# One core of Trainium2: the first output tile placed between the gates' first pair and the pooled products, with weight highs, head seam and pool groups in another order

## Chip, cores and metric

One core of one Trainium2 chip. The metric is the device time in microseconds (us) of one execution. A profiled execution gives the rows; the other times are of runs without a profile.

## What is computed

One step of a streaming encoder layer, in fp32, on 1024 prompt tokens and 32 sample tokens. Cut to what matters:

```
x += 0.5 * post(SwiGLU_1(pre(x)))            # FFN 1, d_ff 2816
h = pre(x); z = h @ W_in                     # q|f|i|og|u|gA|gB, d_model 1024
yA = up_A(gnorm(HGRN2(q, f, i)) * silu(og))  # 8 heads of 128, chunks of 64
yB = up_B(scale * groupwise_linear(trailing_mean_w(u) - u)), w in (2, 4, 8, 16)
x += post(W_out(sigmoid(gA) * yA + sigmoid(gB) * yB))
x += 0.5 * post(SwiGLU_2(pre(x)))            # FFN 2
x += post(sigmoid(pre(x) @ W_pg) * (p @ W_pp))
```

Outputs are the new x and the new recurrent and pooling states, for prompt and sample.

## The kernel before

**Tiles.** Activations lie feature-major, 8 tiles of 128 features, 1056 tokens in four groups `g` of N = 264. An fp32 product is made of f16 halves: each operand is split in a high and a low, and three matmuls of 128x128 by 264 columns (high-high, high-low, low-high; lines 818 to 820 and 849 to 852) stand for one. TensorE issues 20814 matmuls in all.

**Weights** come in units of four 128x128 tiles into a ring of slots. SyncE loads them in the order of use (`load`, `load_pair` at L650), once the slot is free. ScalarE scales a unit by 32 and makes its high half; GpSimd makes its low half. For plain tiles these are `prep` (L1096: scale L1107, high L1109) and GpSimd's `split` (low L719). For pairs they are `scale` (L1144, four raw units), `to_high` (L1154, L1162) and GpSimd's `pair` (L721), which also adds and subtracts raw units (sums L736, lows L732). `first_highs` (L1171) is `to_high` for the first pair of a stage, whose slots were last used by the stage before.

**Plain tiles and pairs.** `turn` (L798) makes plain output tiles, a job per token group. `pair` (L832) makes two columns of output tiles at once by a scheme of seven products in place of eight: each product `k` in two token halves `e` of 12 matmuls, 168 matmuls per pair. Its right-hand operands are sums of activation blocks, `t`, which VectorE adds (`t_block`, L1909), ScalarE rounds to a high half (`t_high`, L1185, L1191) and VectorE subtracts to a low (`t_lows`, L1919). Its results are put together from the seven products in PSUM banks: ScalarE copies some banks (`chain_copies`, L1371), VectorE adds the rest (L1936 in the FFNs, L2027 in the mixer). Each read releases its bank (`bank_read`), and a matmul group waits for the bank that it will fill.

**Stages, in the order of TensorE.** FFN up: 16 plain tiles (first tiles), then 20 pairs; FFN down. Mixer: first head's value, output gate, q and f tiles (head0), 16 pairs for the rest and for the pooling input u, in which the head before is worked on: transposes of values and keys (L931), scores, updates, outputs (L986) stand between products (`head_hooks`, L999). Then pair 0 of the gates, 16 pool tiles of one product each (4 banks), the first outputs (tile 0: 8 blocks by 4 groups, 96 matmuls, from the heads; tile 1: 4 blocks by 4 groups, from the pools), then seven turns of pair and outputs. Then W_out, FFN 2, and the last gate (ple).

**What sets the order.** Each engine has its own program, written out by hand; they meet in semaphores with counted values. The class `Plan` works out banks, uses and slots for each job (`job`, L261), and so what each wait counts to. An engine takes its instructions in order, so an instruction whose input is late holds back all behind it.

**What the change touches.**
- ScalarE: the start (L1673 to L1699: `squares`, `prep`, `norm`, `h_high`, `silus` with its table load at L1141), `up(f)` (L1193), the seam from head0 to the pairs (L1712 to L1726), `head_turn` (L1462), `gates` (L1579) with `pooled_high` (L1564, copy at L1569) and the pooled products' high copies (L1627). `ln_exp_tables` loads the tables for ln and exp.
- VectorE: the start (`h_split` L1778, `square_sum` L1771, `first_squares`, `products`), the seam (L2403 to L2414; `head0_silus` at L2016, `decay_keys` at L2107, `head_turn` L2142 with the scan at L2150 and the key operand at L2125), `gates` (L2322) with `pooling` (L2254, a group of one window; its adds are L2275 for windows 4 and up and L2265 for window 2), `pooled_low` (L2286), the last head's norm (L2112) and low (L2120), `mixed` (L2292, low halves of the pooled products, L2297), `gated` and `joins` (L2303, L2348).
- TensorE: the norms' places in `up(0)` (L1019), `keys_and_values` (L992), and the order of gates, pools and outs (L1042 to L1044).

The order of the pool groups is `POOL_ORDER` (3, 2, 1, 0) for windows 16, 8, 4, 2.

## Time and profile before

| | |
|---|---|
| runs | 2442.74, 2446.56, 2446.6 us; median 2446.56 |
| profiled execution | 2445.24 us |
| its span on the core | 2443.4 us, 54106 instructions |
| mean granted clock of TensorE | 0.983 of full speed |
| busy share | TensorE 96%, weight loads 82%, VectorE 54%, ScalarE 47%, GpSimd 45% |
| the chain that ended last | TensorE 74%, VectorE 9%, issue 8%, GpSimd 5%, ScalarE 3% |
| DMA | 147.26 MB, mean 60 GB/s |

The span is from the first to the last recorded instruction. The granted clock 1.00 is 2.4 GHz, 0.50 is 1.2 GHz. PE is TensorE, DVE VectorE, ACT ScalarE, POOL GpSimd. "L849 <- DVE work L1936" means that the instruction of line 849 waited for a VectorE instruction of line 1936 on the buffer `work`.

### The profile page before, as it was taken

Reading aid. Unit: us, or ns where it says so; the run is one execution under the profiler, and the core shown is the slowest. Engines: PE = TensorE matmul, PEld = TensorE weight load, DVE = VectorE, ACT = ScalarE, POOL = GpSimd, SP = SyncE. Lnnn points to the kernel's source line nnn. Section 1 sums busy time; section 2 is a strip of 40 time slices with the busy share of each in tenths; the row PEclk is TensorE's granted clock in tenths of the full one; section 3 lists DMA queues with packets and bytes.
Section 4 is the critical chain, followed back from the end, with each engine's and each line's share of the span. In section 5 each row is a group of like instructions: output and inputs, shape, how many; then the busy total and the mean of one; then the engine's idle time right before and its main releaser. Section 6 shows DMA issues by size and latency. Waiting matters only on the chain.

```text
span 2443.4 us, 54106 instructions
## 1 busy us (share of the span) xinstructions
PE 2339.7 (96%) x20814; PEld 2004.0 (82%) x20814; DVE 1317.9 (54%) x2273; ACT 1155.7 (47%) x2087; POOL 1111.7 (45%) x881
## 2 busy tenths in 40 slices
PE   7899999999997999999979999988999999999988
PEld 5688888888886888888758888877888888888876
DVE  7655555400189777778952332387666666000755
ACT  6343344333465666666444443653333333334575
POOL 2676777422214555554635443314677776223110
PEclk9999999999998999999989999999999999999999
DMA  3122112322220111111101122321111122321202
GB/s 128 41 59 56 52 56 60 121 53 74 59 85 19 47 46 39 39 51 38 55 23 44 60 60 81 117 80 31 56 52 52 53 58 73 119 70 49 66 18 72
DMA packets 98519, 147.26 MB, mean 60 GB/s; under 512 B 10480, under 2 KB 43504, under 8 KB 98416
## 3 DMA queue, kind: packets, MB, share of 16 engines
q1 hardware_dynamic: 70352, 121.14, 17.1%
q10 hardware_dynamic: 28064, 24.69, 3.1%
q8 instruction: 72, 1.18, 0.2%
q14 instruction: 31, 0.25, 0.0%
HBM read 131.70 MB, written 14.09 MB: 60 GB/s over the span
## 4 chain that ended last, share of the span: by engine, by line
PE 74%; DVE 9%; issue 8%; POOL 5%; ACT 3%; DMA 1%; DVEq 0%; POOLq 0%; ACTq 0%; SPq 0%
PE bank L818 12%; PE bank L849 12%; PE bank L819 12%; PE bank L820 12%; PE bank L852 12%; PE bank L851 12%; POOL ring L732 3%; DVE hid L1974 2%; DVE work L1972 1%; POOL ring L736 1%; DMA ring<-weights 1%; PE bank L975 1%; DVE hid L1785 1%; ACT ring L1148 1%; PE bank L986 1%
## 5 line engine op out<-in xcount | busy, mean ns | idle before, releaser
L849 PE MATMUL bank<-ops,ring 128*128 128x264 f16 x3584 | 994.8, 278 | 34.2 <-DVE work L1936 14.7
L851 PE MATMUL bank<-ops,ring 128*128 128x264 f16 x3584 | 994.0, 277 | 0.0
L852 PE MATMUL bank<-ops,ring 128*128 128x264 f16 x3584 | 994.0, 277 | 0.0
L732 POOL TENSOR_TENSOR ring<-ring 128x512 f16<-128x512 f32 x384 | 484.1, 1279 | 280.7 <-ACT ring L1162 280.7
L818 PE MATMUL bank<-hid,ring 128*128 128x264 f16 x2124 | 587.3, 277 | 0.0
L819 PE MATMUL bank<-hid,ring 128*128 128x264 f16 x2124 | 587.1, 276 | 0.0
L820 PE MATMUL bank<-hid,ring 128*128 128x264 f16 x2124 | 587.0, 276 | 0.0
L719 POOL TENSOR_TENSOR ring<-wtmp,ring 128x512 f16<-128x512 f32 x173 | 203.9, 1181 | 667.4 <-ACT ring L1109 666.3
L849 PEld LDWEIGHTS bank<-ops,ring 128*128 128x128 f16 x3584 | 353.2, 99 | 100.9 <-issue 25.6
L1162 ACT ACTIVATE ring<-ring 128x512 f16<-128x512 f32 x384 | 226.6, 622 | 405.5 <-POOL ring L736 404.0
L852 PEld LDWEIGHTS bank<-ops,ring 128*128 128x128 f16 x3584 | 352.3, 98 | 54.4
L851 PEld LDWEIGHTS bank<-ops,ring 128*128 128x128 f16 x3584 | 352.5, 98 | 52.9
L1811 DVE TENSOR_TENSOR u<-u,work 128x264 f32<-128x264 f32 x112 | 58.3, 521 | 403.7 <-ACT work L1228 402.6
L819 PEld LDWEIGHTS bank<-hid,ring 128*128 128x128 f16 x2124 | 208.2, 98 | 32.8
L818 PEld LDWEIGHTS bank<-hid,ring 128*128 128x128 f16 x2124 | 208.2, 98 | 32.2 <-DVE hid L2297 0.5
L820 PEld LDWEIGHTS bank<-hid,ring 128*128 128x128 f16 x2124 | 208.2, 98 | 31.5
L736 POOL TENSOR_TENSOR wtmp<-ring 128x512 f32<-128x512 f32 x64 | 84.1, 1313 | 306.0 <-ACT ring L1148 306.0
L1148 ACT ACTIVATE ring<-ring 128x512 f32<-128x512 f32 x256 | 148.9, 621 | 152.9 <-DMA ring<-weights 152.6
L818 PE MATMUL bank<-ops,ring 128*128 128x264 f16 x640 | 182.7, 285 | 21.7 <-DVE hid L2016 5.6
L819 PE MATMUL bank<-ops,ring 128*128 128x264 f16 x640 | 182.6, 285 | 0.0
L820 PE MATMUL bank<-ops,ring 128*128 128x264 f16 x640 | 182.4, 285 | 0.0
L736 POOL TENSOR_TENSOR ring<-ring 128x512 f32<-128x512 f32 x128 | 173.3, 1354 | 0.0
(179 smaller groups left out, 2855.7 us busy)
## 6 DMA issues: line engine op xcount, KB each, us to landing
ring<-weights SPq DMA_DIRECT2D x429, 256.0 KB, 2.7
hid<-xT SPq DMA_DIRECT2D x8, 528.0 KB, 8.3
hid<-out_x ACTq DMA_DIRECT2D x8, 528.0 KB, 7.6
out_x<-hid ACTq DMA_DIRECT2D x8, 528.0 KB, 4.2
ops<-xT ACTq DMA_DIRECT2D x6, 528.0 KB, 7.1
out_x<-ops ACTq DMA_DIRECT2D x6, 528.0 KB, 4.2
ops<-out_x ACTq DMA_DIRECT2D x6, 528.0 KB, 6.5
out_x<-ops SPq DMA_DIRECT2D x12, 264.0 KB, 2.2
```

The source lines that it names most:

```text
L719: nc.gpsimd.tensor_tensor(low(slot), wtmp[:, u % 2, :], high(slot), ALU.subtract).then_inc(unit_ready, 1)
L732: nc.gpsimd.tensor_tensor(low(slot), weight_source(name, k), high(slot), ALU.subtract)\
L736: nc.gpsimd.tensor_tensor(out, in0, in1, op).then_inc(wsum_ready, 1)
L818: nc.tensor.matmul(out, whi, rhs(t, k, g, 0), start=(k == 0), stop=False)
L819: nc.tensor.matmul(out, whi, rhs(t, k, g, 1), start=False, stop=False)
L820: mm = nc.tensor.matmul(out, wlo, rhs(t, k, g, 0), start=False, stop=end)
L849: nc.tensor.matmul(out, whi, xhi, start=(kk == 0 and fresh(name, k)), stop=False, skip_group_check=True)
L851: nc.tensor.matmul(out, whi, xlo, start=False, stop=False, skip_group_check=True)
L852: mm = nc.tensor.matmul(out, wlo, xhi, start=False, stop=end, skip_group_check=True)
L1148: nc.scalar.activation(raw(slot), raw(slot), ACT.Copy, scale=WS).then_inc(scaled, 1)
L1162: nc.scalar.activation(high(slot), weight_source(name, k), ACT.Copy).then_inc(whi_ready, 1)
L1811: V_.tensor_tensor(ssq(g), ssq(g), pair_buf[:, n % 2, :], ALU.add).then_inc(ysq_added, 1)
```

## The change

It reorders; no matmul, product or transfer is added or removed, but table loads are (at the start `ln_exp_tables` is also called between silu 0 and silu 1). By part:

- **Gates, TensorE:** pair 0, output tile 0, pools, output tile 1, where it was pair 0, pools, both output tiles. The pools keep their four banks; `Plan.job` counts the uses anew.
- **Gates, ScalarE:** the second and third chain copies stand ahead of most weight preparations; the pooled products' copies stand ahead of the weight highs 3 to 6.
- **Gates, VectorE:** window 2 before window 4; the last head's norm and low ahead of the window-4 group; tile 0's gated product ahead of the pooled lows.
- **FFN up, ScalarE:** weight highs 2 to 6 ahead of late t highs, in both FFNs.
- **Heads' seam:** VectorE's t blocks are cut in two by `head0_silus`; decay keys ahead of the last t lows; weight highs 5 and 6 moved into `head_turn(1)`; value transposes wait for the values alone; the last head unit's order.
- **Start:** preparations and the splits of the first token groups in another order; the second t block's squares of group 2 on VectorE instead of ScalarE; the norms' places.

The diff, cut:

```diff
 HG_FIRST = {k: HG_PIECES.index(k) for k in dict.fromkeys(HG_PIECES)}
-POOL_ORDER = (3, 2, 1, 0)
-HEAD_UNITS = ((4, 5, 2, 3), (2, 3, -4, -3), (6, 7, 4, 5), (-2, -1, -4, -3))
+POOL_ORDER = (3, 2, 0, 1)
+HEAD_UNITS = ((4, 5, 2, 3), (2, 3, -4, -3), (6, 7, 4, 5), (-4, -3, -2, -1))
...
 b = self.banks(name)[pos % STAGES[name]["banks"]]
+if name == "pools":
+    return b, self.base[name][b] + pos // STAGES[name]["banks"] + 1
+if name == "outs" and isinstance(i, int) and i == 0 and pos < G:
+    return b, self.base["pools"][b]
...
             pe.wait_ge(bank_read[b], uses)
-    def turn(name, i, kind, rhs, ready=None, hooks=None, order=None):
+    def turn(name, i, kind, rhs, ready=None, hooks=None, order=None, ts=None):
...
         for pos, (t, g) in enumerate(jobs_of(name, kind)):
+            if ts and t not in ts:
+                continue
...
         pe.wait_ge(operand_ready, head * 8 + n)
-    def keys_and_values(h):
-        pe.wait_ge(k_ready, h)
-        for e in range(2):
-            b, uses = plan.product("heads", h * 2 - 3, 6, e)
+    def values(h):
+        pe.wait_ge(pads_set, 1)
+        for g in range(G):
+            b, uses = plan.head0_job(0, g)
             pe.wait_ge(bank_read[b], uses + 1)
+        for k in (3, 6):
+            for e in range(2):
+                b, uses = plan.product("heads", h * 2 - 3, k, e)
+                pe.wait_ge(bank_read[b], uses + 1)
...
         return [{
-            (0, 1): [lambda: keys_and_values(h), lambda: head_transposes(hh, "vT", V)],
+            (0, 1): [lambda: values(h), lambda: head_transposes(hh, "vT", V)],
...
     norm(0)
-    up(0, {(1, 4): calls(1), (2, 4): calls(2), (5, 0): calls(3)})
+    up(0, {(2, 2): calls(1), (3, 4): calls(2), (7, 0): calls(3)})
...
     pair("gates", 0)
+    turn("outs", 0, "M", out_rhs, first_out_ready, ts=(0,))
     turn("pools", 0, "M", pool_rhs, pool_ready, order=POOL_ORDER)
-    turn("outs", 0, "M", out_rhs, first_out_ready)
+    turn("outs", 0, "M", out_rhs, first_out_ready, ts=(1,))
...
         return freed
-    def t_high(p, n, at):
+    def t_high(p, n, at, es=range(2)):
...
             act.wait_ge(x_saved[g], saves(1, g))
-        for e in range(2):
+        for e in es:
...
         t_high(2 * f, 2, (2, 4))
-        high0(2)
-        silus(f, (6, 7))
-        t_high(2 * f, 3, (5, 6))
-        high0(3)
+        silus(f, (6,))
+        high0(3, 4)
+        silus(f, (7,))
+        t_high(2 * f, 3, (5, 6), (0,))
+        high0(5, 6)
+        t_high(2 * f, 3, (5, 6), (1,))
         t_high(2 * f, 1, (1, 3))
-        high0(4)
         t_high(2 * f, 4, (7, 8))
-        high0(5, 6)
...
             silus(1, (2, 3))
-            first_highs(UPS[1][1])(0, 1)
+            first_highs(UPS[1][1])(0, 1, 2)
...
         exps_32(hh)
-        if not (isinstance(h, int) and h == 1):
+        if isinstance(h, int) and h == 1:
+            first_highs("heads")(5, 6)
+        else:
...
             .then_inc(pool_stored[j], 16)
+    def mixed_high(t):
+        for g in range(G):
+            b, uses = plan.job("pools", 0, t * G + g)
+            act.wait_ge(bank_full[b], uses + 1)
+            nc.scalar.activation(hid[:, MIX0 + POOL_ORDER[t], g, 0:N], bank[b][:, 0:N], ACT.Copy,
+                                 scale=pscale(POOL_ORDER[t])).then_inc(mixed_hi_ready, 1)
...
                     to_high("gates", m + 1, ks, freed)
+            first = isinstance(m, int) and m == 0
             chain_copies("gates", m, 0)
-            if isinstance(m, int) and m == 0:
+            if first:
                 first_highs("gates")(5, 6)
-            prep("outs", m, 0, 1, 2)
-            if not last:
+                chain_copies("gates", m, 2)
+                prep("outs", m, 0)
+                pooled_high(1)
+                prep("outs", m, 1, 2)
+                chain_copies("gates", m, 4)
+                pooled_high(2)
+                onorm_high(HEADS - 1, W[3])
                 scale("gates", m + 1)
-            if isinstance(m, int) and m == 0:
-                pooled_high(1)
-            chain_copies("gates", m, 2)
-            ahead(0, 1)
-            chain_copies("gates", m, 4)
-            if isinstance(m, int) and m == 0:
-                pooled_high(2)
-                pooled_high(3)
-                onorm_high(HEADS - 1, W[3])
+                ahead(0, 1)
             else:
+                prep("outs", m, 0, 1, 2)
+                if not last:
+                    scale("gates", m + 1)
+                chain_copies("gates", m, 2)
+                ahead(0, 1)
+                chain_copies("gates", m, 4)
...
             ahead(2)
+            if first:
+                pooled_high(3)
...
             nc.scalar.activation(dst_b, gb_all, ACT.Sigmoid).then_inc(gate_ready, 1)
+            if first:
+                for t in range(4):
+                    mixed_high(t)
...
         gate_turn(0, TMP_FIRST[0][:, 0:T], TMP_FIRST[1][:, 0:T])
-        for n, (t, g) in enumerate((t, g) for t in range(4) for g in range(G)):
-            b, uses = plan.job("pools", 0, n)
-            act.wait_ge(bank_full[b], uses + 1)
-            nc.scalar.activation(hid[:, MIX0 + POOL_ORDER[t], g, 0:N], bank[b][:, 0:N], ACT.Copy,
-                                 scale=pscale(POOL_ORDER[t])).then_inc(mixed_hi_ready, 1)
...
     norm(0)
-    prep("ffn1_up0", 0, 2, 3)
+    prep("ffn1_up0", 0, 2)
     h_high(0, 0)
+    prep("ffn1_up0", 0, 3, 4)
     squares(0, 1)
-    prep("ffn1_up0", 0, 4)
-    squares(0, 2)
+    prep("ffn1_up0", 0, 5, 6, 7)
     norm(1)
-    prep("ffn1_up0", 0, 5)
     h_high(0, 1)
-    prep("ffn1_up0", 0, 6)
+    silus(0, (0,))
     squares(0, 3)
-    prep("ffn1_up0", 0, 7)
+    ln_exp_tables()
     norm(2)
-    silus(0, (0,))
...
     silus(0, (2, 3))
-    first_highs(UPS[0][1])(0, 1)
+    first_highs(UPS[0][1])(0, 1, 2)
...
     head0_evac(3)
+    t_high(1, 4, (7, 8))
+    high0(4)
     ln_exp_tables()
-    high0(4)
-    t_high(1, 4, (7, 8))
-    high0(5, 6)
...
         sq = hq(p, g)
-        dve.wait_ge(squares_ready, SQUARE_PARTS * (G * p + g + 1))
+        if p or g != 2:
+            dve.wait_ge(squares_ready, SQUARE_PARTS * (G * p + g + (0 if p or g > 2 else 1)))
...
                 .then_inc(h_ready, 1)
-        ahead = 2 if c == 0 else PARTS
+        ahead = min(c + 1, 2) if p == 0 else PARTS
...
                          pooled[j][:, :, 0:N], ALU.subtract).then_inc(pooled_ready, 1)
-    def mixed():
-        for n, (t, g) in enumerate((t, g) for t in range(4) for g in range(G)):
-            b, _ = plan.job("pools", 0, n)
+    def mixed_low(t):
+        for g in range(G):
+            n = t * G + g
+            b, uses = plan.job("pools", 0, n)
...
                                     in1=dst[:, 0:N], op0=ALU.mult, op1=ALU.subtract).then_inc(bank_read[b], 1)
-        dve.wait_ge(bank_read[b], plan.job("pools", 0, n)[1] + 1)
+        return b, uses
+    def mixed(t):
+        b, uses = mixed_low(t)
+        dve.wait_ge(bank_read[b], uses + 1)
...
         pooling(2, 2 * HEADS - 1, 1, 5)
+        onorm(HEADS - 1, W[3], LAST_RMS)
         sums_b_odd("gates", 0, lambda g: gcols(gb_all, g))
+        pooled_low(2)
+        onorm_low(HEADS - 1, W[3])
         pooling(3, 2 * HEADS - 1, 3, 6)
-        onorm(HEADS - 1, W[3], LAST_RMS)
-        pooled_low(2)
...
         pooled_low(3)
-        onorm_low(HEADS - 1, W[3])
-        mixed()
+        first_gated(0, lambda g: gcols(TMP_FIRST[0], g))
+        for t in range(3):
+            mixed_low(t)
+        mixed(3)
...
             gate_sums(m)
+            first_gated(m, lambda g: hidv[:, TMP0, g, :])
...
         sums_b_even("gates", m, lambda g: gcols(gb_all, g))
-    def joins(m, a, s, dst):
+    def first_gated(m, a):
...
             gated(m, 0, g, a(g))
+    def joins(m, a, s, dst):
...
     h_split(0, 0)
+    for n, ks in enumerate(parts_of(SQUARE_PARTS)):
+        x = xk(0, 2, ks.start, ks.stop)
+        dve.wait_ge(x_loaded[2][n], 16)
+        step(V_.tensor_tensor(hq(0, 2)[:, ks, :], x, x, ALU.mult))
     first_squares(1)
-    first_squares(2)
+    square_sum(0, 2)
     h_split(0, 1)
+    products(0, (0,))
     first_squares(3)
-    products(0, (0,))
...
     step(V_.memset(smask.rearrange("p (c t) -> p c t", t=C)[:, :, 0], 0.0))
-    t_block(1, (1, 2))
+    t_block(1, (1, 2), (0,))
     head0_silus(1)
+    t_block(1, (1, 2), (1,))
     t_lows(1, 2)
-    t_block(1, (3,))
+    t_block(1, (3,), (0,))
     head0_silus(2)
+    t_block(1, (3,), (1,))
...
     head0_silus(3)
-    t_lows(1, 4)
...
     decay_keys(0)
+    t_lows(1, 4)
```

## Rows read from the trace of the kernel before

**Rows 1.** The page, part 1: busy time, share of the span, instructions

```profile
PE 2339.7 (96%) x20814; PEld 2004.0 (82%) x20814; DVE 1317.9 (54%) x2273; ACT 1155.7 (47%) x2087; POOL 1111.7 (45%) x881
```

**Rows 2.** Waits of TensorE, whole span: us in total, times, longest us

```profile
PE bank L849 <- DVE work L1936: 14.7, 21, 4.6
PE bank L818 <- DVE hid L2297: 12.1, 1, 12.1
PE bank L849 <- POOL ring L732: 11.9, 4, 3.9
...
PE bank L931 <- DVE hid L2107: 5.8, 1, 5.8
PE bank L818 <- DVE hid L2016: 5.6, 1, 5.6
...
PE bank L849 <- ACT work L1371: 5.2, 8, 2.5
...
PE bank L849 <- DVE work L2027: 2.3, 2, 1.7
```

**Rows 3.** Windows, mid-FFN 1 and 2: us, PE, PEld, DVE, ACT, POOL, clock, DMA, GB/s

```profile
130.00:450.00 320.00, 320.00 (x2847) 278.33 (x2845) 178.37 (x337) 128.23 (x221) 225.24 (x188) 1.00 0.21 60
1731.00:2051.00 320.00, 315.54 (x2783) 270.75 (x2781) 201.38 (x331) 120.92 (x215) 232.37 (x183) 1.00 0.20 56
```

**Rows 4.** Windows: the start, after FFN 1's seam, gates, pools, FFN 2's seam

```profile
0.00:70.30 70.30, 55.11 (x409) 44.38 (x410) 52.02 (x91) 44.99 (x70) 18.77 (x18) 0.93 0.34 115
108.90:114.80 5.90, 5.90 (x28) 4.04 (x29) 2.33 (x7) 2.28 (x4) 3.18 (x3) 0.50 0.14 44
1216.60:1280.00 63.40, 46.53 (x368) 37.42 (x366) 36.83 (x63) 28.11 (x52) 22.23 (x16) 0.87 0.10 30
1256.00:1261.70 5.70, 5.64 (x26) 3.91 (x27) 4.45 (x11) 4.11 (x10) 0.93 (x1) 0.50 0.01 3
1710.80:1714.00 3.20, 3.14 (x28) 2.75 (x29) 2.21 (x7) 1.30 (x3) 0.43 (x1) 1.00 0.31 87
```

**Rows 5.** Timeline of ACT, gates: start, us, line, op, [idle before <- releaser]

```profile
1227.33 2.17 ACT L1148 ACTIVATE ring<-ring 128x512 f32<-128x512 f32 x4
...
1255.01 1.58 ACT L1627 ACTIVATE hid<-bank,col 128x264 f16<-128x264 f32 x4
```

**Rows 6.** Timeline of DVE, gates

```profile
1232.19 4.37 DVE L2275 TENSOR_TENSOR hid<-hid 128x1085 f32<-128x1085 f32 x2
...
1240.10 1.23 DVE L2265 TENSOR_TENSOR hid<-hid 128x1023 f32<-128x1023 f32 x1
...
1255.51 1.69 DVE L2297 SCALAR_TENSOR_TENSOR hid<-bank,col,hid 128x264 f16<-128x264 f32 x4 [8.35 <-ACT hid L1627]
```

**Rows 7.** Timeline of ACT, seams from first tiles to pairs in both FFNs

```profile
82.20 2.25 ACT L1191 ACTIVATE ops<-hid 128x1056 f16<-128x1056 f32 x2 [5.45 <-DVE hid L1909]
...
91.27 0.63 ACT L1148 ACTIVATE ring<-ring 128x512 f32<-128x512 f32 x1 [4.22 <-DMA ring<-weights]
...
99.98 0.63 ACT L1169 ACTIVATE work<-work 128x528 f32<-128x528 f32 x1
...
1693.31 0.63 ACT L1148 ACTIVATE ring<-ring 128x512 f32<-128x512 f32 x1 [5.92 <-DMA ring<-weights]
```

**Rows 8.** Timeline of DVE, FFN 1, first pair

```profile
108.30 0.76 DVE L1936 COPY work<-bank 128x264 f32<-128x264 f32 x2
```

**Rows 9.** Timeline of DVE, heads' seam

```profile
734.57 7.03 DVE L1909 TENSOR_TENSOR hid<-hid 128x1056 f32<-128x1056 f32 x4
...
761.13 3.58 DVE L1919 TENSOR_TENSOR ops<-hid,ops 128x1056 f16<-128x1056 f32 x2 [1.56 <-ACT ops L1191]
...
767.55 2.42 DVE L2150 TENSOR_TENSOR_SCAN hid<-u,hid 128x1088 f32<-128x1088 bf16 x1 [1.27 <-ACT hid L1408]
...
774.57 1.27 DVE L2125 TENSOR_TENSOR hid<-hid 128x1088 f32<-128x1088 f32 x1
```

**Rows 10.** Timeline of ACT, start

```profile
48.65 1.28 ACT L1141 ACT_TABLE_LOAD   x1
```

## The prediction made before the change was run

> **What bounds the kernel now.** I read the page first: TensorE is busy for 2339.7 us, 96% of the span [rows 1], so only what keeps it waiting or slow can be won; no matmul is added or removed. The list of its waits comes next [rows 2]. The largest single one, 12.1 us, is for the VectorE line L2297 (low halves of the mixed pool products). Two more kinds lie in the same stage: 2.5 us at most for a ScalarE chain copy (L1371), and 2.3 us in two waits for L2027. The waits of 11.9 us for GpSimd's L732 and of 14.7 us for VectorE's L1936 lie where the FFNs go from their first tiles to their pairs; 5.8 us (L2107) and 5.6 us (L2016) lie where the heads begin. Third, the windows at mid-FFN [rows 3]: in 320 us the first FFN issues 2847 matmuls without a pause and the second only 2783. A matmul is 320/2847 = 0.1124 us; a pair of 168 takes 18.9 us in FFN 1 and 18.9 x 2847/2783 = 19.3 us in FFN 2. Fourth, the granted clock [rows 4]: after the long waits TensorE works at 0.50 (1.2 GHz), where each busy us costs 0.5 us. So a stall has two prices.
>
> **Gates (products of pair 0, pools, first outs).** Before, this takes 1216.6 to 1280.0, 63.4 us [rows 4]. Its 360 matmuls (14x12 + 16x3 + 4x24 + 4x12) need 40.5 us, so 22.9 us are lost: 16.9 in waits (12.1 + 2.5 + 2.3) and 6.0 in slow clock.
> - ScalarE before: three weight preparations, four scalings (2.17 us, row 1227.33 [rows 5]) and a pooled copy stand ahead of the copies of product 2, so product 4 starts 2.5 us late. The change puts these copies first; one preparation of 1.3 us and a pooled copy of 1.1 follow, then two more preparations. They end near 1230, just before product 4's first half does. The 2.5 and its slow clock go.
> - VectorE before: the window-4 pool group (its adds alone 4.37 us, row 1232.19 [rows 6]) stands ahead of the late sums of product 3's bank. Now the window-2 group, with one difference of 1.23 us (row 1240.10 [rows 6]), comes first: 1.7 us go, I keep 0.3. The 0.54 us wait behind the window-8 group stays.
> - The 12.1 us: the pool products start at once but only four banks exist, and the copies that free them come on ScalarE after seven weight highs, at 1255.01 [rows 5]. After the change TensorE does the first output tile first, 96 matmuls, 10.8 us, from 1236.4 to 1247.2. It needs the last head's split: the norm and its low half move ahead of the window-4 group and end near 1236.1, product index 7 wants it at 1237. The third pooled copy and the window-4 group (5 to 7 us of VectorE) lie under the 10.8 us.
> - Then the pools. Each tile needs a 0.49 us ScalarE copy and a VectorE op of the same size, at a pitch of 0.4 (row 1255.51 [rows 6]), against 0.34 us on TensorE. From the first tile's end 1.1 us pass to the first bank, 16 x 0.4 to the last: the second output tile starts near 1254.8, not 1252.6. Price 2.3 us.
> Sum: 22.9 - 0.5 - 0.3 - 2.3 = 19.8; I take **19.5**, bounds 15 (head split late, or slow clock in the pools) and 21. Queues: SyncE gets the pool unit and the outs units in the same order; the pool weight slots are loaded long before.
>
> **FFN seams.** Before, the chain in FFN 1 is: the second-block copies (L1191) end at 84.45; two highs follow, whose lows free the last raw slot; its load lands and is scaled at 91.27 [rows 7]; GpSimd's sums take 7.5 us; the silu is at 99.98 [rows 7]; VectorE then makes the hidden tile and copies the next product at 108.30 [rows 8]. TensorE waits 3.9, 1.2 and 4.6 us. With highs 3 to 6 moved ahead, slots are free and loaded before 84; the four scalings (2.1 us) run at once, with less GpSimd contention in the t blocks about 1 us earlier: scaled by 85.3, not 91.9. The whole chain moves 6.7 us. TensorE is then early: it stalls at most 1 us for the first weights of pair 1, and 4.7 us for L1936. So the last wait stays, and with it its slow clock (6 us at 0.50 before [rows 4], 3 us lost); I take it alike. Whether the start is worth more is below; with its slow clock I take **5.8** for start and seam of FFN 1, bounds 2 and 8.
> In FFN 2 the order is the same, but its load landed later (scaled from 1693.31 [rows 7]), so the chain moves 8.3 us. Its last wait was only 3.0 us and the clock stayed full (1710.8 to 1714.0 at 1.00 [rows 4]). I see in this why its pairs take 19.3 us: VectorE's hidden tile then falls on GpSimd's lows at once, L1936 is late in each pair (8 us over the FFN). FFN 1, put back 3 us by its slow clock, runs clear of it. With a wait of 4.7 us FFN 2 should get the slow clock (-3 us) and afterwards FFN 1's pace (+8.1 = 18 x 0.45). Sum 8.3 - 3.0 + 8.1 = **13.4**, bounds 6 and 16.
>
> **Heads' seam.** VectorE does four t sums, 7.03 us, before the silus that free TensorE's bank [rows 9]. Two stay ahead, 3.5 us go. The rest of the t chain hangs on GpSimd's sums and comes only some 1 us earlier. The first head's value transposes no longer wait for L2107: 5.8 us go at that place. But the key transposes wait for the operand at 774.57, which comes from decay keys, log, scan (767.55 [rows 9]). The decay keys now precede the last two lows (3.58 us [rows 9]), and two highs leave ScalarE's way: the scan starts at 762 to 763, the operand is done near 771.3 instead of 775.9. TensorE is there at 766.3: a wait of 5 us takes the place of the other two, and slow clock after it, 2.8 us. 4.6 - 2.8 = **1.8**, bounds 0 and 6. In the seven looped turns the added waits are for reads long done; TensorE shows no wait there but the chain copies of 0.2 to 0.5 us: nothing. A cover gone would cost up to 1 us a turn.
>
> **Start.** Earlier lows start TensorE 1.3 us sooner, and preparations put first remove its waits for the weights; it would reach the second group 5 us earlier. But ScalarE now has two more table loads (1.28 us each, row 48.65 [rows 10]) and all of h's copies later, so silu 2 ends near 53.7, not 50.3. Tile 10 wants its bank at 70.3 - 6 x 2.7 = 54.1 before [rows 4], at 50.6 now: it waits 3 us. Gain 0.4, perhaps minus 1.7 of slow clock. The Trainium skill, "ScalarE: Activation LUTs", What happens when an exp ACTIVATE runs, gives a table load about 2.7 us; at that the start alone would lose 2.5 us more, while the row says 1.28.
>
> **Sum.** 19.5 + 5.8 + 13.4 + 1.8 = 40.5 us. The profiled execution took 2445.2 (span 2443.4), 1.3 below the median of 2446.56; differences carry over: 2446.6 - 40.5 = **2406**.
>
> **Rivals.**
> - *FFN 2 keeps its slow pace* (the stall is short or the clock stays full): 8.3 - 1.2 = 7 instead of 13.4, or FFN 1 falls into it as well; 2413. For it: this is what FFN 2 does now. Against: every wait of 3.9 us or more here was followed by slow clock. Chance 0.20.
> - *Seams give nothing*, each wait moved to the next link with its clock; only gates: 2425. For: three of my seam sums already end in such a wait. 0.09.
> - *The first output tile waits for the last head or bank*, so nothing is filled: 2446 within 0.2%. Against: its operands are ready before in my walk. 0.03.
> - *Slower: GpSimd and VectorE collide in every FFN pair.* Place: GpSimd's five lows and sum against VectorE's hidden tile. Ops of 1.25 us take up to 2.2 when they meet (7.03 for four [rows 9]). Had all five met, the weight loop would be 18.4 + 5 = 23 us against 18.9; it decides once the loop exceeds the present pace by 1.1 us a pair (38 pairs eat 40 us), fully met about 2560. Against: rows 3 show 19.3 at worst. 0.04. The Trainium skill, "SBUF — State Buffer", SBUF: two separate sides, says that VectorE ops with two SBUF inputs and GpSimd's lock a shared port pair for a whole instruction; by that alone each of the five could wait a full op.
> - *The table load at the page's price*: 2409; 0.02. The remaining 0.02 is a gain above 50.
>
> **Numbers.** Forecast 0.60. Likeliest 2406, own range 2398 to 2411. The range takes in the slow-pace case and most of the third: 2396 to 2423. Over 0.2% (5 us, about what a measurement tells) faster: 0.60 + 0.20 + 0.09 + 0.02 + 0.02 = 0.93; same 0.03; slower 0.04.
>
> **What would show it.** Gates: no wait for L2297 over 1 us; pair 0 to pair 1 about 44 us. FFN seams: no wait for L732 over 1 us, one wait of 4 to 5 us for L1936 in each, both followed by 0.50; then 2847 matmuls in 320 us in both. Heads: value transposes without a wait, key transposes late by about 5. Start: tile 10 waits some 3 us. Wrong it would be if GpSimd's lows in the pairs lengthen, if head 7's split is what TensorE waits for at the first output tile, or if clock below 1 shows where no wait stands.

## The result and the profile after

The changed kernel takes 2424.64 us (median of 4 runs, 2423.38 to 2426.86) against 2446.58 (2442.74 to 2448.64): a ratio of 0.9915, 95% interval 0.9899 to 0.9930. That is 21.9 us faster where 40.5 were forecast, and 1.6 us above the upper end of the range. The profiled execution took 2425.5 us, its span is 2423.6.

The page of the changed kernel, part 1, answers to [rows 1]:

```profile
PE 2336.5 (96%) x20814; PEld 1998.0 (82%) x20814; DVE 1361.7 (56%) x2275; ACT 1151.5 (48%) x2087; POOL 1131.4 (47%) x881
```

VectorE has two instructions more and is busy 43.8 us longer; GpSimd has none more and is busy 19.7 us longer. The same work takes longer; why is the subject of the section on the two rhythms. TensorE's waits of the changed kernel (us in total, times, longest) answer to [rows 2]:

```profile
PE bank L856 <- DVE work L1962: 14.1, 37, 2.4
PE bank L856 <- DVE work L1982: 8.1, 2, 4.3
...
PE bank L825 <- ACT work L1154: 5.2, 2, 2.9
...
PE bank L938 <- DVE hid L2151: 4.0, 1, 4.0
...
PE bank L825 <- DVE hid L2342: 1.0, 1, 1.0
```

L1962 is L1936 of before (VectorE's copy of product 0 of the next pair), L1982 VectorE's sum of product 4, L1154 the silus of the first tiles, L2342 the new line of tile 0's gated product. The 12.1 us for the pooled lows, the 2.5 for L1371 and the 11.9 for GpSimd's lows are gone. But the copy of product 0 is now waited for 37 times, not 21. The windows answer to [rows 3] (both FFNs, shifted as the FFNs are) and to the gates' window of [rows 4]; columns as there:

```profile
130.00:450.00 320.00, 314.84 (x2777) 270.06 (x2776) 201.91 (x330) 120.00 (x213) 231.66 (x182) 1.00 0.20 56
1711.00:2031.00 320.00, 316.09 (x2788) 271.15 (x2786) 201.09 (x330) 121.90 (x216) 233.61 (x184) 1.00 0.19 57
```

```profile
1223.10:1267.40 44.30, 41.04 (x353) 32.76 (x352) 38.70 (x60) 26.63 (x50) 22.55 (x16) 1.00 0.13 41
```

FFN 1 had 2847 matmuls in 320 us; it now has 2777, as few as FFN 2. The gates' stretch takes 44.3 us in place of 63.4, at full clock.

TensorE has 20814 matmuls in both kernels, and outside the gates in the same order. So the n-th can be set against the n-th, and the difference of their starts says where time went:

```
part (numbers of TensorE's matmuls)        forecast   traces (changed minus before)
start (0 to 504)                            -0.4        +5.3
FFN 1's seam (504 to 672)                   -5.4        -6.9
FFN 1's pairs (672 to 3864)                  0         +10.1
heads' seam (6048 to 7392)                  -1.8        -2.1
gates, pools, outs (10584 to 11256)        -19.5       -19.1
FFN 2's seam (14448 to 14616)               -5.3        -6.5
FFN 2's pairs (14616 to 17640)              -8.1        -0.6
rest                                         0          +0.1
sum                                        -40.5       -19.8
```

Four of seven terms are right within 1.5 us. What fails is the pairs of both FFNs (17.6 us in all) and the start (5.7 us). The rest is a sum of two parts that no term had: 1.7 us less between the gates and FFN 2 (matmuls 11256 to 14448) and 1.6 us more behind FFN 2's pairs; in both a stretch at 0.50 is there in one of the two executions and missing or shorter in the other.

Each row comes from one execution of each kernel. Where the other kernels below hold the same code, their executions tell how far such a number moves. The start of matmul 504 lies between 85.5 and 87.2 us in the six with the changed start, and between 81.0 and 81.6 in the five with the start as before. The heads' seam wins 1.0 to 4.0 us. The gates' part wins 19.1 us where the clock stays at 1.00 behind a wait of 3.0 us at the heads' end (the changed kernel, e5, e6, e9, e11, e13 to e15), 17.4 where it falls to 0.50 for 3.4 us there (e1, e3, e10, e12), and 16.1 to 16.2 where it falls for 6.8 us (e2, e7, e8).

### The profile page after: what moved, and what is told of

Its sections match the earlier page's. It is cut to its first block, busy times and chain, and to the rows that moved or that the text cites. A ratio compares the mean times of both kernels' runs of the same rounds, so it can differ in the third digit from the quotient of the medians.

```text
span 2423.6 us, 54141 instructions
## 1 busy us (share of the span) xinstructions
PE 2336.5 (96%) x20814; PEld 1998.0 (82%) x20814; DVE 1361.7 (56%) x2275; ACT 1151.5 (48%) x2087; POOL 1131.4 (47%) x881
## 4 chain that ended last, share of the span: by engine, by line
PE 69%; DVE 13%; issue 9%; POOL 4%; ACT 3%; DMA 1%; DVEq 1%; POOLq 0%; ACTq 0%; SPq 0%
PE bank L825 11%; PE bank L826 11%; PE bank L827 11%; PE bank L856 11%; PE bank L859 10%; PE bank L858 10%; DVE hid L2000 4%; DVE work L1998 3%; POOL ring L737 2%; DVE hid L1811 1%; POOL ring L741 1%; PE bank L982 1%; DMA ring<-weights 1%; ACT ring L1161 1%; PE bank L938 1%
## 5 line engine op out<-in xcount | busy, mean ns | idle before, releaser
L737 POOL TENSOR_TENSOR ring<-ring 128x512 f16<-128x512 f32 x384 | 490.8, 1297 | 261.5 <-ACT ring L1175 261.5
```

What stands on the lines that cost most here:

```text
L737: nc.gpsimd.tensor_tensor(low(slot), weight_source(name, k), high(slot), ALU.subtract)\
```

## Two rhythms of the FFN pairs

One pair in the fast rhythm, kernel before, FFN 1: timelines of VectorE and of GpSimd (start, us, line and operation).

```profile
274.32 0.70 DVE L1972 SCALAR_TENSOR_TENSOR work<-work 128x528 f32<-128x528 f32 x1
275.18 1.15 DVE L1974 TENSOR_SCALAR hid<-work 128x528 f32 x1 [0.16 <-DVE work L1972]
276.47 1.44 DVE L1975 TENSOR_TENSOR hid<-work,hid 128x528 f32 x1
277.83 0.69 DVE L1972 SCALAR_TENSOR_TENSOR work<-work 128x528 f32<-128x528 f32 x1
278.68 0.44 DVE L1974 TENSOR_SCALAR hid<-work 128x528 f32 x1
279.25 0.71 DVE L1975 TENSOR_TENSOR hid<-work,hid 128x528 f32 x1
```

```profile
274.82 2.53 POOL L732 TENSOR_TENSOR ring<-ring 128x512 f16<-128x512 f32 x2 [0.74 <-ACT ring L1162]
281.12 1.27 POOL L736 TENSOR_TENSOR wtmp<-ring 128x512 f32<-128x512 f32 x1 [3.78 <-ACT ring L1148]
```

These six VectorE operations make the hidden tile, in two halves; GpSimd's are the lows and sums of the next pair's weights. The hidden tile takes 5.64 us, its second half falls into GpSimd's pause, and the next sum of raw weights starts 6.8 us after the tile's start (281.12 - 274.32). This span is called the distance from here on. The loop that makes the weights of the next pair (load, ScalarE's scaling and highs, GpSimd's sums and lows) is called the weights' loop. The same pair in the changed kernel:

```profile
276.61 1.02 DVE L1998 SCALAR_TENSOR_TENSOR work<-work 128x528 f32<-128x528 f32 x1
277.79 1.14 DVE L2000 TENSOR_SCALAR hid<-work 128x528 f32 x1 [0.16 <-DVE work L1998]
279.08 1.55 DVE L2001 TENSOR_TENSOR hid<-work,hid 128x528 f32 x1
...
282.70 1.44 DVE L2001 TENSOR_TENSOR hid<-work,hid 128x528 f32 x1
284.06 0.76 DVE L1962 COPY work<-bank 128x264 f32<-128x264 f32 x2
```

```profile
277.02 1.62 POOL L737 TENSOR_TENSOR ring<-wtmp,ring 128x512 f16<-128x512 f32 x1
278.60 1.45 POOL L741 TENSOR_TENSOR ring<-ring 128x512 f32<-128x512 f32 x1
280.80 2.77 POOL L737 TENSOR_TENSOR ring<-ring 128x512 f16<-128x512 f32 x2 [0.74 <-ACT ring L1175]
287.34 1.26 POOL L741 TENSOR_TENSOR wtmp<-ring 128x512 f32<-128x512 f32 x1 [3.77 <-ACT ring L1161]
```

```profile
284.61 0.28 PE L856 MATMUL bank<-ops,ring 128*128 128x264 f16 x1 [0.28 <-DVE work L1962]
```

Both halves now meet GpSimd. The tile takes 7.53 us, the copy behind it comes late, and TensorE waits for it. The distance is 10.7 us. An operation of 0.44 us takes 1.14 and one of 0.71 takes 1.55 when they meet; GpSimd's low takes 1.62, not 1.16. The operations at 277.79 and 279.08 end 0.3 and 0.6 us after the GpSimd operation beside each has ended (278.64, 280.05). This is so in every pair looked at: in the changed kernel from 130 to 440 us all 32 operations of L2000 end 0.29 us after the GpSimd operation under which they began, and all 32 of L2001 end 0.56 to 0.57 us after it. Each is its undisturbed time (0.44 and 0.71 us) less about 0.15 us. The Trainium skill, "SBUF — State Buffer", SBUF: two separate sides, calls the shared port pair an exclusive lock, held for a whole instruction; these ends agree with it.

The numbers of the distance and the tile in all four FFN runs:

```
                    distance   hidden tile   pair
before, FFN 1       6.7-6.9     5.64         18.90 (from pair 2)
before, FFN 2       10.5-10.9   7.4-7.8      19.2-19.6
changed, FFN 1      10.5-10.9   7.4-7.7      19.2-19.5
changed, FFN 2      10.5-10.9   7.4-7.7      19.2-19.6
```

What sets the distance? In the kernel before, FFN 1 starts at 10.9 too; 22.48 us pass to its second hidden tile, which stands at 6.8. In between lie the wait of 4.63 us for the copy (104.23) and 6.8 us at 0.50 (from 108.01), both behind the start of the first hidden tile (100.64). The reading is that they held TensorE and VectorE back, and not the weights, which had been started. In the changed kernel the long wait is for product 4 (4.34 us at 88.90, clock 0.50 from 92.31), ahead of the first silu. The silus and the weights' highs share ScalarE's queue, so both loops would shift together.

By the matmuls' numbers the wait stands where one stood before. At matmul 526 TensorE waited 3.89 us for GpSimd's lows; now it waits 4.34 us there for VectorE. The waits of 1.22 us at matmul 574 and 4.63 us at 646 are gone (0.17 us are left at 646). In FFN 2, matmul 14478 waited 3.89 us for the lows and now waits 3.72 us for VectorE; 2.87 us at 14526 are gone, and 2.95 us at 14598 became 1.74. VectorE came late because its own queue was full: from 60 us to 93.5 us no gap in it is over 0.04 us, and the fourth t block (L1935) and its lows (L1945) stand ahead of the sum:

```profile
87.41 2.41 DVE L1935 TENSOR_TENSOR hid<-hid 128x1056 f32<-128x1056 f32 x2
89.74 0.76 DVE L1977 TENSOR_TENSOR work<-bank,work 128x264 f32<-128x264 f32 x2
90.42 2.41 DVE L1945 TENSOR_TENSOR ops<-hid,ops 128x1056 f16<-128x1056 f32 x2
92.76 0.76 DVE L1982 TENSOR_TENSOR work<-bank,work 128x264 f32<-128x264 f32 x2
```

The theory: a delay of TensorE behind pair 0's silus decides the rhythm. The rival: the order of the weight highs does.

## Experiments on the pairs

Each ratio is to the kernel before, measured beside the run. The changed kernel has 0.9915 [0.9899, 0.9930]; of the experiments only e5 and e8 have an interval that lies wholly below this one. The total time of the others that are built on the changed kernel does not tell them from it, and the argument rests on their traces; e4 is built on the kernel before and compared with that.

**e3: a delay added.** 32 matmuls, written over by the next one; nothing else changes.

```diff
-                pair(rest, 0, t_wait(p))
+                pair(rest, 0, t_wait(p), pad={(6, 0): 32})
...
+                        for _ in range((pad or {}).get((k, e), 0)):
+                            nc.tensor.matmul(out, ring[:, slot, 0:P], ops[:, e, k, 0, 0:N], start=True, stop=False,
```

> The changed kernel with 32 more matmuls (3.6 us) ahead of product 6 of pair 0, in both FFNs, written over by the next one: a single delay of TensorE and of VectorE's hidden tile against the weights' loop. Theory of two rhythms: the distance from the hidden tile to GpSimd's next sum falls from 10.7 to 7.1 us or less and stays there, the pairs go at 18.9 us and not 19.4, and the time falls by 2 x (0.5 x 19 - 3.6), about 11 us, to 2413. Rival (the pace comes from the order of the weight highs or from the slots): the pairs stay at 19.4 us and the time rises by up to 7.2 us, to 2431.8.

2416.75 us (2413.64 to 2426.20), ratio 0.9892 [0.9862, 0.9923]; windows of e3:

```profile
130.00:450.00 320.00, 320.00 (x2847) 278.33 (x2845) 188.73 (x339) 123.07 (x218) 231.36 (x187) 1.00 0.20 59
1711.00:2031.00 320.00, 320.00 (x2847) 278.33 (x2845) 189.27 (x340) 127.33 (x225) 231.80 (x188) 1.00 0.21 61
```

The median is 7.9 us under the changed kernel's; one of the four runs (2426.20) lies among the changed kernel's, and the intervals overlap. The trace is plain: with 64 matmuls more both FFNs go without a pause, at 18.90 us per pair. The order of the weight highs is the changed kernel's, so the rival falls. The distance starts at 7.6 us, where 7.1 or less was expected, and creeps to 8.5 by FFN 1's pair 17; the tile grows with it from 5.7 to 6.9 us. So this distance does not hold by itself. The runs spread over 12.6 us.

**e4: the same delay in the kernel before, FFN 2 alone.**

> The kernel before with the same 32 matmuls in pair 0 of FFN 2 alone. Theory of two rhythms: FFN 2 goes at 18.9 us per pair as FFN 1 does; -8.1 + 3.6, about 4.5 us less: 2442. Rival: FFN 2 stays at 19.35 us per pair and the time rises to 2450.

2444.8 us (10 runs, 2439.76 to 2448.29), ratio 0.9992 [0.9981, 1.0004]: no difference that counts. In the profiled execution (2441.73 us) the delay works: the distance is 7.8 and grows to 9.9 at pair 15, the pairs take 18.90 up to there and 19.3 behind it. Between the same matmuls FFN 2's seam takes 1.7 us more and its pairs 5.9 less, 4.2 in all. The median of the ten runs does not show this. That the fast rhythm was lost earlier in others would explain it, but they have no trace.

**e11: the seams' order undone** (weight highs 3 to 6 in both FFNs as before, rest as changed).

> The changed kernel with the order of weight highs at both FFNs' seams as before. Theory: the seams cost 6.9 and 6.5 us again, but the wait of 4.6 us for the copy of pair 1 and the slow clock behind it come back behind the first hidden tile, delay TensorE against the weights' loop, and both FFNs go at 18.9 us per pair: 10 and 8 us less. Net 4 to 5 us less than the changed kernel, about 2420. Rival (the rhythm does not hang on where the seam's wait falls): both stay at 19.4 us and the time rises to 2438.

2422.97 us, ratio 0.9915 [0.9898, 0.9932]: the ratio of the changed kernel itself. The medians differ by 1.7 us, where 4 to 5 were expected and the runs spread over 4.8. Its waits:

```profile
PE bank L856 <- DVE work L1961: 11.7, 3, 4.6
PE bank L856 <- POOL ring L737: 7.8, 2, 3.9
```

Both waits of 4.6 us are back behind the first hidden tile, and both FFNs go at 18.90: FFN 1 at distance 7.8, lost in the last three pairs; FFN 2 from 7.8 down to 6.7, where it holds. From nearly one distance it may go either way. (The same holds in e1 below: its FFN 1, with the code of the kernel before, stands at 7.95 in its second pair and not at 6.8, and loses the fast rhythm after pair 15.)

What holds 6.7 is a wait of ScalarE. In the kernel before, FFN 1, the first silu of each pair waits 0.2 to 0.4 us for TensorE's product (through VectorE's L1959):

```profile
270.45 0.64 ACT L1169 ACTIVATE work<-work 128x528 f32<-128x528 f32 x1 [0.32 <-DVE work L1959]
```

e11's FFN 2 shows the same once it stands at 6.7. At distances from 7.6 to 8.5 (e3 in both FFNs, e11's FFN 1) and at 10.7 (the slow rhythm in both kernels) the silus of these pairs wait for nothing, so the weights' loop is free to drift there.

By the matmuls' numbers the seam gives back 6.6 us and FFN 1's pairs win 8.0. So the seams' part of the change, which won 13.4 us at its place, is worth about nothing as a whole.

**e1: the gates' part alone,** on the kernel before.

> The kernel before with the gates' part alone (order of TensorE, ScalarE and VectorE there, pool groups, last head unit). If the gates' gain is its own, TensorE's time is alike up to the gates and 19 to 19.6 us less behind them: about 2427.5 us. Rival: the gates' gain hangs on where the heads end, and the last head's order costs in the heads what it gives here; then under 15 us.

2421.53 us, ratio 0.9902 [0.9874, 0.9930]: one part of the change does as much as all of it. At the gates it wins 17.4 us, less than the 19.1 in the whole; the 1.7 between them is a stretch of 3.4 us at 0.50 at the heads' end (from 1213.13), which comes in this execution and not in the other, behind the same wait of 3.0 us. The 6 us under the expected 2427.5 come from FFN 2, whose code is that of the kernel before: at matmul 14598 it waited 4.62 us for the copy, not 2.95, the clock was at 0.50 for 6.8 us, and its pairs went at 18.90, 7.6 us less.

**e6: VectorE's copies of the next pair between the halves of the hidden tile.**

> The changed kernel with VectorE's copies of the next pair's product 0 between the two halves of the hidden tile, in both FFNs, the weights' loop as it was. TensorE then no longer waits for those copies. If the copy behind the hidden tile is the whole bound, all pairs go at 18.9 us: about 2406. If the weights' loop is a bound of its own at 19.4 us, the distance from hidden tile to sum grows by 0.45 us per pair from 10.7, and after some ten pairs TensorE waits for GpSimd's lows in each pair instead: about 2415. Rival (neither counts): 2424.6.

2426.18 us, ratio 0.9920 [0.9897, 0.9943]. In the looped pairs no copy is waited for any more, but L2002 (product 4) is:

```profile
PE bank L856 <- DVE work L2002: 14.8, 29, 4.3
```

The distance stays at 10.6 to 10.9, it does not grow, and the pairs take 19.3: the tile now starts when the silu ends (276.61), and the silu stands in ScalarE's queue behind weight high 3, which waited 4.0 us for GpSimd's sum (to 275.35). So the weights' loop looks like a bound of its own, which reaches TensorE by the silu and VectorE, not by the lows as I had expected. e5 puts this to the test.

**e5: a shorter weights' loop.**

```diff
-                    scale(name, i + 1)
-                    to_high(name, i + 1, range(4), product_before(name, i))
+                    scale(name, i + 1, (0, 2, 1))
+                    to_high(name, i + 1, (0, 1), product_before(name, i))
+                    scale(name, i + 1, (3,))
+                    to_high(name, i + 1, (2, 3), product_before(name, i))
...
+                if early:
+                    lo(0)
+                    lo(1)
                 pool.wait_ge(scaled, p * RAWS + (sums + 4))
```

> The changed kernel with a shorter weights' loop in the FFN pairs: ScalarE makes highs 0 and 1 before it scales the last raw unit, and GpSimd their lows before its two sums, so 2.3 us of GpSimd's work lie under the 3.7 us in which it waits for the last load. No delay is added. If the slow rhythm lives on a weights' loop that takes 19.4 us by itself, the loop now takes about 17.1, runs up against the silus, and all pairs go at 18.9 us with a hidden tile of 5.6 to 6.5 us: 19 x 0.5 in each FFN, about 2406 us. Rival: VectorE's hidden tile is slowed wherever the loop stands and TensorE still waits 0.45 us for the copy in each pair: 2424.6.

2414.5 us, ratio 0.9875 [0.9852, 0.9898]. ScalarE and GpSimd in e5:

```profile
270.15 0.64 ACT L1187 ACTIVATE work<-work 128x528 f32<-128x528 f32 x1 [1.20 <-DVE work L1992]
```

```profile
277.77 1.48 POOL L737 TENSOR_TENSOR ring<-ring 128x512 f16<-128x512 f32 x1 [0.72 <-ACT ring L1180]
279.86 1.55 POOL L737 TENSOR_TENSOR ring<-ring 128x512 f16<-128x512 f32 x1 [0.61 <-ACT ring L1180]
281.38 1.26 POOL L741 TENSOR_TENSOR wtmp<-ring 128x512 f32<-128x512 f32 x1
```

The silu now waits 1.2 us for TensorE's product (through L1992) in each pair, so the loop has slack and cannot drift, as at 6.7 above but with more room: from pair 3 on the distance is 7.34 to 7.36, the tile 6.37, the pair 18.90, in both FFNs. Lows 0 and 1 lie ahead of the sum. It wins 10.1 us on the changed kernel and not 18.6: the first two pairs still go at 19.4 to 19.6, the wait for the copy at pair 1 is 2.3 us, and by the matmuls' numbers the pairs of FFN 1 and FFN 2 give 8.0 and 7.0 us, less 0.6 at each seam.

**e8: e5 with the start as before.**

> The shorter weights' loop together with the start as before. If both gains are their own, 4.4 us (the start) and 2 x 9.5 us (the rhythm) go from 2424.6: about 2401, below both kernels. Rival: one eats the other (the first pair's wait grows by what the start gives), 2406.

2408.14 us (2406.40 to 2409.11), ratio 0.9845 [0.9822, 0.9868]: 16.5 us less than the changed kernel, the best of all, though 7 us short of the expected 2401, as e5 was. The two gains do not eat each other (10.1 and 3.9 alone, 16.5 together).

## Experiments on the start and the heads

**e2: the start as before.**

> The changed kernel with the start as before (ScalarE's and VectorE's start and the places of the norms undone). Theory A: the start's 5.3 us are a loss of their own; TensorE ends its first tiles 5 us earlier and the time falls to about 2419.5. Rival B: the first pair hangs on VectorE's t chain anyway; then the wait at FFN 1's first pair (4.3 us now) grows by most of 5 us and the time stays within 1.5 us of 2424.6.

2420.7 us, ratio 0.9894 [0.9871, 0.9917]: 3.9 us less. TensorE reaches matmul 504 4.8 us earlier, and the wait at the first pair does not grow (3.2 us, not 4.3): the loss is its own.

What in it costs? ScalarE in the changed kernel at the silus:

```profile
46.46 0.64 ACT L1141 ACTIVATE ops<-hid 128x528 f16<-128x528 f32 x1 [1.16 <-DVE hid L1811]
47.12 1.28 ACT L1154 ACT_TABLE_LOAD   x1
...
54.95 0.64 ACT L1141 ACTIVATE ops<-hid 128x528 f16<-128x528 f32 x1 [0.77 <-DVE hid L1811]
55.62 1.28 ACT L1154 ACT_TABLE_LOAD   x1
56.91 0.67 ACT L1154 ACTIVATE work<-bank 128x264 f32<-128x264 f32 x2
```

Silus 2 and 3 stood at 49.94 before, behind the load of [rows 10]; now at 56.91. Six kernels take the start apart (all else as changed; the numbers are TensorE's start of matmul 504 in us, 86.26 in the changed kernel, 80.99 in the one before; by the spread given above, differences under some 1.5 us say nothing):

**e7: silu 0 and its tables back.**

> The changed kernel with silu 0 behind the third norm again and without the added table call; the rest of the start stays as changed. If the start's 5.3 us come from the two added table loads (1.28 us each) and what they push back, TensorE's waits for the silus (2.3 and 2.9 us) fall to one of under 2 us and 4 to 5 us come back at the end of the first tiles: 2420. If they come from the late copies of h, less than 2 us come back: 2423 or more. The pairs stay at 19.4 us in both.

87.7, and 2426.95 us (0.9926 [0.9903, 0.9948]). The loads alone are not it.

**e9: group 1's norm early,** though group 2's squares and sum still stand ahead of group 1's split on VectorE, so the copies of h came only 0.6 us earlier (31.54).

> The changed kernel with token group 1's norm early again: its squares ahead of preparations 3 and 4, its sum on VectorE ahead of group 2's squares, the norms' places on TensorE as before; silus, tables and group 2's squares on VectorE stay as changed. If the start's loss comes from the copies of h, which run 5.5 us late from group 1 on (32.14 against 26.61), 4 us or more come back before the first pair and the time falls to 2420 or less. If it comes from the silus' places and their tables, the copies come early but TensorE waits for a silu as before: 2424.

87.7, and 2427.0 us (0.9930 [0.9914, 0.9947]); the edit missed its aim, TensorE waited 5.2 us for GpSimd's lows.

**e12: group 1 wholly first.**

> The changed kernel with token group 1 wholly ahead of group 2 at the start: on VectorE its sum and its split stand ahead of group 2's squares and sum (5.9 us in the last try, where they stood between the two), on ScalarE its squares and norm ahead of the preparations. If those 5.9 us are what makes the copies of h late, group 1's copies start at 27 to 28 us and not at 32.1, and TensorE ends its first tiles 3 to 5 us earlier: 2420 to 2421. Rival: the preparations, now behind, hold the first tile's later units, TensorE waits for GpSimd's lows (L724) instead, as it did for 5.2 us in the last try, and under 1 us comes back.

87.7, and 2425.44 us (0.9918 [0.9902, 0.9935]): its rival holds. The copies start as wanted, but GpSimd's two lows take 4.23 us beside VectorE's splits and squares, and TensorE waits 6.6 us for them:

```profile
27.82 0.64 ACT L1141 ACTIVATE ops<-hid 128x528 f16<-128x528 f32 x1 [0.95 <-DVE hid L1811]
```

```profile
32.74 4.23 POOL L724 TENSOR_TENSOR ring<-wtmp,ring 128x512 f16<-128x512 f32 x2 [7.83 <-ACT ring L1122]
```

**e13: group 2's squares back on ScalarE. e14: silu 0 and tables too. e15: the norms' places too.**

> The changed kernel with group 2's squares on ScalarE again (right behind group 1's) and VectorE's start as before. If VectorE's added squares hold the start back, TensorE reaches the middle of pair 0 (its 504th matmul, 86.3 us) 3 us earlier or more; if the loss hangs on silu 0 and the tables together with them, only the next kernel shows it, and here it is under 1.5 us.

> As the last one, and silu 0 behind the third norm again without the added table call. If both edits together hold the loss (each alone is hidden by the other), 4 us or more of the 5.3 come back at the same matmul; if it is the preparations or the norms' places, no more than in the last one.

> As the last one, and the norms at their old places on TensorE; only the order of ScalarE's weight preparations is still the changed one. If the late norms hold the copies of h back, the rest of the 5.3 us comes back here; if the preparations ahead of norm 1 do it, TensorE still comes 2 us late or more and only the whole undo (81.0 to 81.5 us at the same matmul) has it.

85.8, 83.7 and 84.0, and 2425.99, 2422.25 and 2423.86 us (3, 3 and 3 runs; 0.9913 [0.9891, 0.9936], 0.9896 [0.9873, 0.9918], 0.9899 [0.9876, 0.9921]). So about half of the loss sits in the squares and the silu's tables together, each of which alone gives nothing that can be told from the spread; the norms' places give nothing; the other half (83.7 to 84.0 against 81.5 in e2) is in what is left, the preparations put ahead of group 1's norm and VectorE's order of full tiles and lows (the line `ahead = min(c + 1, 2)`, which the expectations of e13 and e15 overlook). Which of the two it is stays open.

**e10: the heads' seam as before.**

> The changed kernel with the heads' seam as before. TensorE's time from the start of the first head tiles to the second head grows by 2 us (what the two traces show between the same matmuls), nothing else moves: 2426.6. Rival: the seam's waits are filled by what is late anyway, no difference over 0.5 us.

2426.99 us (0.9934 [0.9918, 0.9951]). By the matmuls' numbers 1.9 us come back from 6048 to 6384, as expected; the 2.3 of the medians is of the size of the runs' spread. But against the executions of e2, e5 and e11, with the same seam as the changed kernel, it is only 0.9: there the wait for L2151 is 5.7 us and not 4.0, and one of 2.5 us for ScalarE's line L1360 is added; against the largest (e12) it is 3.7. So the seam does win, and how much hangs on the execution.

## Why the prediction was wrong

- **Gates, right.** "I take 19.5": 19.1, of which 16.1 hold and 3.0 hang on whether, and for how long, the clock falls at the heads' end. The first output tile filled the wait. The price of 2.3 us for the pools came as drawn: 1.0 us from the first tile's end to the first bank (L2342), and 1.3 us behind the pools' last step.
- **Seams, right in size, wrong in place.** 5.4 and 5.3 us were forecast, 6.9 and 6.5 came. But the step "So the last wait stays, and with it its slow clock" failed. The first wait stayed (4.3 us in FFN 1, 3.7 in FFN 2), in pair 0 ahead of the silu, and the last one shrank (0.2 and 1.7 us). The prediction moved the weights' chain ahead and left out VectorE's queue of t blocks and lows, which reaches product 4's sum at 92.8 us only. That the sizes agree within 1.5 us is in part luck: one long wait is left either way, in FFN 1 with 6.8 us at 0.50 behind it.
- **The pairs, the failed step.** "With a wait of 4.7 us FFN 2 should get the slow clock (-3 us) and afterwards FFN 1's pace (+8.1 = 18 x 0.45)." The mechanism in it is shown by e3, e11 and e1's FFN 2: a delay of TensorE at the end of pair 0 does bring 18.90. What it left out is what keeps the pace: a silu that waits for TensorE. Its condition was not met in either FFN, because the stall stood ahead of pair 0's silu. The first rival named this ("FFN 2 keeps its slow pace ..., or FFN 1 falls into it as well") and was priced at 2413, with FFN 2 alone; with FFN 1's 10.1 us it would have been 2423. A chance of 0.20 was too small for something that one wait's place decides in both FFNs. The range ended at 2423, below the price of the second rival too (2425).
- **The start, wrong sign.** "Gain 0.4": a loss of 5.3. The wait of 3 us at tile 10 came (2.9), but it began at 54.4 us and not at 50.6: "it would reach the second group 5 us earlier" failed. TensorE had first waited 2.8 us at a norm (L886, from 25.2) and 2.3 us for silu 1 (from 46.5), which the term left out; silu 2 ended at 57.3, where 53.7 was forecast. The table loads took 1.28 us each, and the ACTIVATE behind each began 0.01 us after its end, so the rival of a dearer load did not come.
- **Heads, right in size, in part by luck.** 1.8 forecast, 2.1 measured here and 1.0 to 4.0 in other executions. The path was drawn with one wait of 5 us; there are three, 2.1 and 2.6 us for L2042 and 4.0 for L2151 (the key transposes).
- The rival on the slower side, collisions in every pair, named the right two engines; it is what happened to FFN 1's pairs, at 0.5 us a pair, where 4 to 5 were its worst case.

## What to carry to other kernels

Where two loops of nearly one length share a resource (here what VectorE's and GpSimd's operations hold each other up by), find their distance in time before and after a change: a stall that is taken away, or moved ahead of the point where the loops part, may be what kept them apart. Look for which loop has slack in each round; a good rhythm held where the loop beside the bottleneck waited for it in each round (FFN 1 before, e5), and drifted where the two merely missed each other (e3, e4). And judge each part of a bundle alone: here the gates' part gave all that the bundle gave. The part of a gain that comes from a clock that happened to stay up, or a rhythm that happened to hold, has to be looked for in more than one execution.

## What the runs showed of the hardware

- Work side by side on VectorE and GpSimd slows both: a copy with rounding from 0.44 to 1.14 us, a low from 1.16 to 1.62, and at the start of e12 GpSimd's lows to 2.1 or 2.2 us each beside VectorE operations of 1.25 us that took 2.1.
- A VectorE operation that begins under a GpSimd one ends a fixed time after it: 0.29 us for L2000, 0.56 to 0.57 us for L2001, in all 64 cases counted.
- Behind equal waits of 3.0 us, at the same place, the granted clock fell to 0.50 for 3.4 us in the kernel before and in e1, for 6.8 us in e2 and e8, and stayed at 1.00 in the changed kernel. Differences of 1.7 to 3.0 us between single executions can be this alone.
- A rhythm of two loops is not fixed by the code alone: the same FFN 2 went at 19.3 us per pair in the kernel before and at 18.90 in e1.
